# Leaving out the dummy matmuls that fill TensorE's waits in a two-block kernel

## The chip, the cores and the metric

The kernel runs on one NeuronCore of a Trainium2 chip, as one launch that computes the whole model. The metric is the device time of one execution in microseconds (us).
## The reference, cut to what matters

256 tokens of width 1024 pass through a first block of two layers and a second block of one layer. Between the parts stand RMS norms, and at those the matmuls have to wait, since each needs the norm of the whole row:

```python
for l in range(DEPTH):                       # first block, DEPTH = 2
    h = rmsnorm(x, g_mix[l])
    ... = jnp.split(h @ w_in[l], split_at, axis=-1)
    ...                                      # three kinds of attention
    x = x + jnp.concatenate([o_a, o_b, o_c], axis=-1) @ w_out[l]
    hf = rmsnorm(x, g_mlp[l])
    x = x + jnp.square(jax.nn.relu(hf @ w_ff1[l])) @ w_ff2[l]
x = rmsnorm(x, g_final)
# second block
p = rms_norm(x, norm1_gain) @ w_in
...                                          # attention, and the recurrent part (wkv7_scan)
o = (o + bonus) * g                          # end of the recurrent part
y_rwkv = o @ w_rwkv_out
mixed = gates[..., :D] * y_att + gates[..., D:] * y_rwkv
x = x + mixed @ w_out
x = x + hierarchical_moe(rms_norm(x, norm2_gain), ...)   # 32 experts, top 2
```

## The kernel before

Each engine has its own program, written out in order; semaphores tie them together. The two layers of the first block are a hardware loop (`for l`); the second block follows in straight code, and the experts (`hierarchical_moe`) are a last loop.

**A norm and its turn.** ScalarE takes the sums of squares (L1589, L1592), VectorE the reciprocals and the scaled rows (L2022, L2025), and signals `xn_ready` (`xn2_ready` in the second block). TensorE then turns the rows with 16 `transposes` (L965) into four PSUM banks (stages `tr1`, `tr2`, `tr3`). In the first block and at the entry of the second, ScalarE copies each bank out as a rounded high part (L1619) and VectorE forms the low part from it (L1633); `wait_emptied` makes TensorE wait for the last bank. Only then come the products.

**Split products.** The wide matmuls of the first block and of the second's projections are made of three passes (L984, L985, L986) over high and low parts of both operands. The weights' parts are made beforehand by ScalarE (L1645) and GpSimd or VectorE (L865), in queues that they share with the norms' work. The later matmuls of the second block, `token_major` (L974), are plain fp32; each fp32 matmul with a plain operand leaves two records in the trace.

**The filling.** `bridge(pe, units, key, n)` takes the bank of the stage named by `key` and issues n matmuls of 128x256 that read constants and whose result is overwritten by the stage's own first matmul (L956). They stand on TensorE's queue:

- in each layer ahead of `tr1` (18) and behind it (9), ahead of `tr3` (13) and behind it (4);
- at the entry of the second block, ahead of its `tr1` (28);
- ahead of `oT` (18), the turning of the recurrent part's result `o`, which waits for `o_ready`; `yrw`, the product with `w_rwkv_out`, follows;
- ahead of `mixT` (6), which waits for `mixed`; the product with `w_out` follows;
- ahead of `tr2` (10), the last norm; the router's small product `route`, the choice of experts on VectorE and the gathering of rows (L1517) follow, and then the experts' loop, whose first stage is `gate` (L1550).

A bridge has no semaphore of its own beyond the bank's: it is a fixed amount of work ahead of the wait, so TensorE looks at the wait only when the bridge is through. In all 88 matmuls stand in the two layers and 62 in the second block.

**The experts' weights.** The experts' matrices (2 MB each, `w_expert_gate`, `_up`, `_down`) go through single slots: SP issues the load of the next one (L941) when TensorE has finished the stage that read the slot.

Of the kernel before, what the change touches and what calls it, by code (L numbers as in the profile page):

```python
# [27 lines left out]
SEQ, D = 256, 1024  # L28
# [538 lines left out]
def program(nc, io, out):  # L567
    tables = shape_tables()
    with ExitStack() as ctx:
# [52 lines left out]
        def shared(name):  # L622
            o, w = shared_at[name]
            return shared_c[:, o:o + w]
# [9 lines left out]
        ident, causal = shared("ident"), shared("causal")  # L634
# [8 lines left out]
        proj = area(0, T * IN_W).rearrange("p (t w) -> p t w", t=T)  # L643
# [63 lines left out]
        oT = hTs[:, 1024:2048].rearrange("p (k s) -> p k s", k=4)  # L707
# [240 lines left out]
            sp.dma_start(out[0].rearrange("(t p) d -> p t d", p=P), x).then_inc(out_stored, 16)  # L948
            sp.wait_ge(out_stored, 16)

        def bridge(pe, units, key, n):

            bank = units.begin(key)
            for _ in range(n):
                pe.matmul(bank[:, 0:SEQ], ident, shared("causal")[:, 0:SEQ], start=True, stop=True)  # L956

        def transposes(pe, units, stage, src):

            for j in range(4):  # L960
# [17 lines left out]
        def _(pe):  # L978
# [39 lines left out]
            with pe.Fori(0, DEPTH) as l:  # L1018
                units = UnitView(LU, pe, psum, l)
# [72 lines left out]
                    if last_of_piece:  # L1092
                        read(("out", c, i), ins)

                bridge(pe, units, ("tr1", 0), 18)
                xn_ready.wait(pe, T, l)
                transposes(pe, units, "tr1", xn)
                bridge(pe, units, ("proj", 0), 9)
                units.wait_emptied(*(("tr1", j) for j in range(4)))
                for b in range(3):  # L1100
                    project_in(b, 0)
# [3 lines left out]
                for t in range(T):  # L1105
                    bank = units.begin(("idxT", t))
# [6 lines left out]
                for t in range(T):  # L1113
                    bank = units.begin(("dsaT", t))
# [19 lines left out]
                for t in range(T):  # L1134
                    bank = units.begin(("retT", t))
# [6 lines left out]
                for i, (t, s, h0) in enumerate(RET_UNITS):  # L1142
                    bank = units.begin(("retS", i))
# [12 lines left out]
                for t in range(T):  # L1156
                    bank = units.begin(("retO", t))
                    for h in range(RET_H):
                        mine = [i for i, u in enumerate(RET_UNITS) if (u[0], u[2]) == (t, h % 2)]
                        for i in mine:  # L1160
# [3 lines left out]
                                            start=(i == mine[0]), stop=(i == mine[-1]))  # L1164
# [15 lines left out]
                for j in range(4):  # L1180
                    t, c0 = j // 2, 4 * (j % 2)
                    bank = units.begin(("mlaT", j))
# [3 lines left out]
                for j in range(4):  # L1186
                    t, c0 = j // 2, 4 * (j % 2)
                    units.wait_emptied(("ukv", T * (j % 2) + t))
                    bank = units.begin(("mlaT", 4 + j))
# [8 lines left out]
                for g in range(N_DSA, NG + 2):  # L1198
# [4 lines left out]
                    n = g - N_DSA  # L1203
# [21 lines left out]
                for t in range(T):  # L1225
                    project_out(1, 0, t, range(4), t == T - 1)

                bridge(pe, units, ("tr3", 0), 13)
                xn_ready.wait(pe, 3 * T, l)
                transposes(pe, units, "tr3", xn)  # L1230
                bridge(pe, units, ("ff1", 0), 4)
                units.wait_emptied(*(("tr3", j) for j in range(4)))

                def ff1(b):
# [29 lines left out]
            units = UnitView(SU, pe, psum)  # L1264
# [6 lines left out]
            _, _, _, part2 = split_products(PW, units, hTp2, second_piece, 0)  # L1271

            def project(stage, blocks):
                for b, (_, w) in enumerate(blocks):
                    for i in range(4):
                        part2(stage, (stage, b, i), [(T * b, slice(0, w))], 2 * i, i == 0, i == 3)

            bridge(pe, units, ("tr1", 0), 28)
            pe.wait_ge(xn2_ready, T)
            transposes(pe, units, "tr1", xn2)  # L1280
            units.wait_emptied(*(("tr1", j) for j in range(4)))
# [4 lines left out]
            bank, r = units.begin(("bias", 0)), slice(0, BUCKETS + ATT_H)  # L1286
            units.finish(("bias", 0), pe.matmul(bank[0:ATT_H, 0:384], bias_tab[r, :], second("bucket_hot")[r, :],
                                                start=True, stop=True))
# [3 lines left out]
            for t in range(T):  # L1292
                bank = units.begin(("loraT", t))
# [5 lines left out]
            for t in range(T):  # L1299
                c = slice(t * P, (t + 1) * P)  # L1300
                for j, r in enumerate((slice(0, LORA_W), slice(LORA_W, P))):
                    bank = units.begin(("lora", 3 * t + j))
                    units.finish(("lora", 3 * t + j), pe.matmul(bank, loraT[r, 0, c], lora_w[r, 0, :], start=True, stop=True))
                bank, rest = units.begin(("lora", 3 * t + 2)), slice(0, LORA_G - P)
# [6 lines left out]
            for j in range(6):  # L1311
                bank = units.begin(("qkT", j))
# [6 lines left out]
            for i in range(NA + 2):  # L1319
                if i < NA:  # L1320
                    t, hg = ATT_UNITS[i]
                    bank, nk = units.begin(("S", i)), (t + 1) * P
                    r = slice(ATT_E * (hg % 2), ATT_E * (hg % 2 + 1))
                    per_bank = 512 // SEQ if t else GRP
                    for g0 in range(0, GRP, per_bank):
# [3 lines left out]
                        for g in range(g0, g1):  # L1329
                            c = (g * HPG + hg) // 2  # L1330
                            ins = pe.matmul(bank[:, g * nk:(g + 1) * nk], qT[r, c, t * P:(t + 1) * P], kT[r, c, 0:nk],
                                            start=False, stop=(g == g1 - 1))
                    units.finish(("S", i), ins)
                if 1 <= i <= NA:
                    t = ATT_UNITS[i - 1][0]
                    pe.wait_ge(att_exp, i)
                    bank = units.begin(("PT", i - 1))
# [123 lines left out]
                        ins = pe.matmul(o, bufK[:, 0, cols], pf[:, 0, C_V + c * P:C_V + (c + 1) * P], start=False, stop=True)  # L1461
                    units.finish(("state", 0), ins)

            bridge(pe, units, ("oT", 0), 18)
            pe.wait_ge(o_ready, 1)
            for j in range(2):
                bank = units.begin(("oT", j))
# [7 lines left out]
            for u in range(2 * T):  # L1475
                t, c = u // 2, u % 2
                token_major(pe, units, ("yrw", u), lambda k: oT[:, k, t * P:(t + 1) * P], w[:, :, c * 512:(c + 1) * 512])
            bridge(pe, units, ("mixT", 0), 6)
            pe.wait_ge(mixed, 1)
            transposes(pe, units, "mixT", gates[:, :, 0:D])  # L1480
            units.wait_emptied(*(("mixT", j) for j in range(4)))
# [2 lines left out]
                for t in range(T):  # L1484
                    token_major(pe, units, ("wout", T * c + t), lambda k: hT[:, k, t * P:(t + 1) * P], w)

            bridge(pe, units, ("tr2", 0), 10)
            pe.wait_ge(xn2_ready, 2 * T)
            transposes(pe, units, "tr2", xn2)
            units.wait_emptied(*(("tr2", j) for j in range(4)))  # L1490
# [1172 lines left out]
```

## Time and profile before

| | before |
|---|---|
| median of 3 runs | 1681.44 us |
| lowest, highest | 1679.95, 1683.43 us |
| the profiled execution | 1682.91 us, of which the span (first to last instruction) is 1681.1 us |
| mean granted clock of TensorE | 0.966 |
| TensorE busy | 1564.4 us (93%) |
| VectorE, ScalarE, GpSimd busy | 707.1, 539.6, 450.2 us |
| dummy matmuls (L956) | 150 matmuls, 300 records |
| DMA, last third of the span | about 428 GB/s, 9 tenths of the 16 DMA engines or more |

A row of a timeline is: start in us, duration in us, engine, source line, operation, output and inputs, and how many instructions the row merges; in brackets stands the idle time of that engine before the row and what ended it. The end of the last matmul of a row is modelled, so a spacing is better taken from starts.

### The profile page before, as it was taken

The numbers are of one execution on the slowest core, as the hardware profiler recorded it, in microseconds if no ns is written. First come the engines' busy times: TensorE is split into PE (matmuls) and PEld (weight loads), VectorE is DVE, ScalarE is ACT, GpSimd is POOL, SyncE is SP. The second block draws the span as 40 slices with busy tenths as digits, with TensorE's granted clock in tenths as the row PEclk, the third lists the DMA queues.
The fourth block names the chain that finished last, engine by engine and source line by source line (L and its number), as shares of the span: only waits on it lengthen the run. The fifth ranks groups of instructions, "written<-read, shape, count | busy, mean of one in ns | idle before, by whom it ended". The sixth has DMA issues, their size and how long they took to land.

```text
span 1681.1 us, 22339 instructions
## 1 busy us (share of the span) xinstructions
PE 1564.4 (93%) x8602; PEld 1156.4 (69%) x8602; DVE 707.1 (42%) x1087; ACT 539.6 (32%) x820; POOL 450.2 (27%) x159
## 2 busy tenths in 40 slices
PE   7979899999979999998989989999799999999997
PEld 6767799998768799986866769975453434344343
DVE  2866365563875365553145735721321111211112
ACT  4546433334646443333435431101111111111010
POOL 3453334333462333434887311100000000000000
PEclk9989999999999999998989999979899999999999
DMA  5432245533432255545654500003499999999994
GB/s 189 163 119 76 101 137 190 200 131 141 163 119 76 101 176 184 182 174 163 202 200 142 214 24 32 1 1 123 180 421 428 428 428 428 429 429 428 428 429 187
DMA packets 44547, 351.79 MB, mean 209 GB/s; under 512 B 5059, under 2 KB 7023, under 8 KB 19887
## 3 DMA queue, kind: packets, MB, share of 16 engines
q1 hardware_dynamic: 43774, 349.35, 54.1%
q8 instruction: 55, 0.90, 0.2%
q10 hardware_dynamic: 576, 1.12, 0.2%
q0 software_dynamic: 112, 0.17, 0.1%
q14 instruction: 30, 0.25, 0.0%
HBM read 347.70 MB, written 1.07 MB: 207 GB/s over the span
## 4 chain that ended last, share of the span: by engine, by line
PE 61%; DMA 18%; DVE 9%; issue 5%; ACT 3%; DVEq 2%; POOL 1%; ACTq 0%; SPq 0%; POOLq 0%
DMA ring<-in_w_expert_up 17%; PE psum L984 12%; PE psum L986 12%; PE psum L985 12%; PE psum L1550 8%; PE psum L974 3%; PE psum L956 1%; PE psum L1576 1%; DVE arena L2025 1%; PE psum L1517 1%; PE psum L1050 1%; PE psum L1419 1%; DVE arena L2070 1%; PE psum L1069 1%; DVE h_split L1633 1%
## 5 line engine op out<-in xcount | busy, mean ns | idle before, releaser
L865 POOL TENSOR_TENSOR weights_split<-weights_raw,weights_split 128x2048 fp32r<-128x2048 f32 (+4 forms) x108 | 392.2, 3644 | 470.6 <-ACT weights_split L1645 470.4
L1645 ACT ACTIVATE weights_split<-weights_raw 128x2048 fp32r<-128x2048 f32 (+5 forms) x156 | 243.5, 1565 | 327.2 <-PE psum L986 326.8
L1550 PE MATMUL psum<-ring,arena 128*64 128x512 f32 x1024 | 225.5, 593 | 25.8 <-DMA ring<-in_w_expert_up 24.7
L1550 PEld LDWEIGHTS psum<-ring,arena 128*64 128x64 f32 x1024 | 73.4, 137 | 174.6 <-issue 174.6
L984 PE MATMUL psum<-weights_split,h_split 128*128 128x512 f32 (+3 forms) x464 | 181.0, 390 | 9.6 <-DVE arena L2287 6.8
L986 PE MATMUL psum<-weights_split,h_split 128*128 128x512 f32 (+3 forms) x464 | 178.0, 384 | 0.0
L985 PE MATMUL psum<-weights_split,h_split 128*128 128x512 f32 (+3 forms) x464 | 177.7, 383 | 0.0
L984 PE MATMUL psum<-h_split,weights_split 128*128 128x256 f32 x512 | 145.0, 283 | 0.8 <-DVE h_split L1633 0.8
L986 PE MATMUL psum<-h_split,weights_split 128*128 128x256 f32 x512 | 144.9, 283 | 0.0
L985 PE MATMUL psum<-h_split,weights_split 128*128 128x256 f32 x512 | 144.9, 283 | 0.0
L984 PE MATMUL psum<-weights_split,hidden_split 128*128 128x512 f32 (+1 forms) x320 | 125.9, 393 | 13.7 <-DVE hidden_split L1633 13.7
L985 PE MATMUL psum<-weights_split,hidden_split 128*128 128x512 f32 (+1 forms) x320 | 125.0, 391 | 0.0
L986 PE MATMUL psum<-weights_split,hidden_split 128*128 128x512 f32 (+1 forms) x320 | 124.6, 389 | 0.0
L865 DVE TENSOR_TENSOR weights_split<-weights_raw,weights_split 128x2048 fp32r<-128x2048 f32 (+2 forms) x48 | 109.4, 2287 | 31.9 <-ACT weights_split L1645 31.2
L1576 PE MATMUL psum<-arena 128*64 128x512 f32 x512 | 113.4, 595 | 0.0
L984 PEld LDWEIGHTS psum<-weights_split,h_split 128*128 128x128 f32 x464 | 90.0, 194 | 29.4 <-issue 10.9
L986 PEld LDWEIGHTS psum<-weights_split,h_split 128*128 128x128 f32 x464 | 89.6, 193 | 17.6
L985 PEld LDWEIGHTS psum<-weights_split,h_split 128*128 128x128 f32 x464 | 89.9, 194 | 16.2
L984 PEld LDWEIGHTS psum<-h_split,weights_split 128*128 128x128 f32 x512 | 98.2, 192 | 2.1 <-issue 1.6
L985 PEld LDWEIGHTS psum<-h_split,weights_split 128*128 128x128 f32 x512 | 98.2, 192 | 0.5
L986 PEld LDWEIGHTS psum<-h_split,weights_split 128*128 128x128 f32 x512 | 98.2, 192 | 0.0
L2228 DVE TENSOR_TENSOR hidden_split<-arena,hidden_split 128x512 fp32r<-128x512 f32 x32 | 86.1, 2691 | 15.8 <-ACT hidden_split L1790 15.8
(354 smaller groups left out, 2157.3 us busy)
## 6 DMA issues: line engine op xcount, KB each, us to landing
weights_raw<-in_layer_w SPq DMA_DIRECT2D x94, 1024.0 KB, 4.8
ring<-in_w_expert_gate SPq DMA_DIRECT2D x32, 2048.0 KB, 16.1
ring<-in_w_expert_up SPq DMA_DIRECT2D x32, 2048.0 KB, 17.1
arena<-in_w_expert_down SPq DMA_DIRECT2D x32, 2048.0 KB, 13.4
weights_raw<-in_second_w SPq DMA_DIRECT2D x44, 512.0 KB, 4.3
weights_raw<-in_layer_w SPq DMA_DIRECT2D x6, 768.0 KB, 4.1
ring<-in_w_out SPq DMA_DIRECT2D x2, 2048.0 KB, 17.0
ring<-in_w_rwkv_out SPq DMA_DIRECT2D x1, 2048.0 KB, 9.7
```

The source lines that it names most:

```text
L865: eng.tensor_tensor(W.part(j, 1, n), W.raw(j, n), W.part(j, 0, n).bitcast(F32), ALU.subtract).then_inc(W.lo[W.pieces[j][1]], 1)
L956: pe.matmul(bank[:, 0:SEQ], ident, shared("causal")[:, 0:SEQ], start=True, stop=True)
L974: ins = pe.matmul(bank[:, 0:n], lhs(i), w[:, i, :], start=(i == 0), stop=(i == k - 1))
L984: pe.matmul(out, a[0], b[0], start=first, stop=False)
L985: pe.matmul(out, a[0], b[1], start=False, stop=False)
L986: return pe.matmul(out, a[1], b[0], start=False, stop=last)
L1050: pe.matmul(bank[:, j * nk:(j + 1) * nk], qT_, kT_, start=True, stop=False)
L1069: ins = pe.matmul(bank[:, j * MLA_V:(j + 1) * MLA_V], probsT[g % 2][:, c * P:(c + 1) * P], v, start=(s == 0), stop=(s == t))
L1550: ins = pe.matmul(bank[half(j), :], xe[h][:, k, half(j)], w[j][:, k, :], start=(k == 0), stop=(k == KD - 1))
L1576: ins = pe.matmul(bank[half(j), :], hidT[:, f, half(j)], w[j][:, f, c * 512:(c + 1) * 512], start=(f == 0), stop=(f == D_EXP // P - 1))
L1645: act.activation(W.part(j, 0, w), W.raw(j, w), ACT.Copy).then_inc(W.hi, 1)
L2228: dve.tensor_tensor(part[1], hid_sq[i % 4], part[0].bitcast(F32), ALU.subtract).then_inc(hid_ready.sem, 1)
```

## The change

Every call of `bridge`, and the function, are taken out. Nothing else is written differently: the waits, transposes and products stand in the same order, and the queues of the other engines hold the same instructions. TensorE is idle where the dummy matmuls were. (Line numbers behind the function shift by 7 and more in the changed kernel.)

```diff
-        def bridge(pe, units, key, n):
-            bank = units.begin(key)
-            for _ in range(n):
-                pe.matmul(bank[:, 0:SEQ], ident, shared("causal")[:, 0:SEQ], start=True, stop=True)
...
-                bridge(pe, units, ("tr1", 0), 18)
                 xn_ready.wait(pe, T, l)
                 transposes(pe, units, "tr1", xn)
-                bridge(pe, units, ("proj", 0), 9)
                 units.wait_emptied(*(("tr1", j) for j in range(4)))
...
-                bridge(pe, units, ("tr3", 0), 13)
                 xn_ready.wait(pe, 3 * T, l)
                 transposes(pe, units, "tr3", xn)
-                bridge(pe, units, ("ff1", 0), 4)
                 units.wait_emptied(*(("tr3", j) for j in range(4)))
...
-            bridge(pe, units, ("tr1", 0), 28)
             pe.wait_ge(xn2_ready, T)
...
-            bridge(pe, units, ("oT", 0), 18)
             pe.wait_ge(o_ready, 1)
...
-            bridge(pe, units, ("mixT", 0), 6)
             pe.wait_ge(mixed, 1)
...
-            bridge(pe, units, ("tr2", 0), 10)
             pe.wait_ge(xn2_ready, 2 * T)
```

TensorE's queue at the head of a layer, before: the loop's head, the bridge of 18, the transposes of the norm, the bridge of 9, and the first split product.

```order
L1018 UNCONDITIONAL_BRANCH
L956 MATMUL psum<-shared_c 128x256 x18
L215 ISA
L965 MATMUL psum<-shared_c,arena 128x128 x16
L956 MATMUL psum<-shared_c 128x256 x9
L129 ISA
L274 ISA
L984 MATMUL psum<-weights_split,h_split 128x512
```

The same place now (the transposes are L958, the products L977):

```order
L1011 UNCONDITIONAL_BRANCH
L1011 ISA
L958 MATMUL psum<-shared_c,arena 128x128 x16
L129 ISA
L274 ISA
L977 MATMUL psum<-weights_split,h_split 128x512
```

Only the two rows of L956 are gone; the transposes stand first, behind their wait.

TensorE's queue from the end of the recurrent part to the router, before (L1454 recurrent part, L1471 `oT`, L974 in turn `yrw`, `wout`, `route`):

```order
L1454 MATMUL psum<-arena 128x64
L956 MATMUL psum<-shared_c 128x256 x18
L1471 MATMUL psum<-shared_c,arena 128x128 x8
L974 MATMUL psum<-ring,hTs 128x512 x16
L956 MATMUL psum<-shared_c 128x256 x6
L965 MATMUL psum<-shared_c,arena 128x128 x16
L974 MATMUL psum<-ring,hTs 128x512 x32
L956 MATMUL psum<-shared_c 128x256 x10
L965 MATMUL psum<-shared_c,arena 128x128 x16
L974 MATMUL psum<-arena,hTs 128x36 x16
```

And now:

```order
L1442 MATMUL psum<-arena 128x64
L1458 MATMUL psum<-shared_c,arena 128x128 x8
L967 MATMUL psum<-ring,hTs 128x512 x16
L958 MATMUL psum<-shared_c,arena 128x128 x16
L967 MATMUL psum<-ring,hTs 128x512 x32
L958 MATMUL psum<-shared_c,arena 128x128 x16
L967 MATMUL psum<-arena,hTs 128x36 x16
```

Three rows of L956 are gone, and each set of transposes stands directly behind the products before it.

## Rows read from the trace of the kernel before

**Rows 1.** Timeline of SP: the first load that reuses an expert's slot.
```profile
1212.02 0.80 SPq L941 DMA_DIRECT2D ring<-in_w_expert_gate  x2
```
**Rows 2.** Chain that ended last: start us, us, what; in the experts' loop.
```profile
1273.90 21.58 DMA ring<-in_w_expert_up
```
**Rows 3.** TensorE by stretch: us, PE busy (instructions), granted clock, DMA share, GB/s.
```profile
202.00:203.00 1.00, 0.02 (x1) 0.80 0.46 74
206.00:207.00 1.00, 1.00 (x8) 0.99 0.01 0
208.50:388.00 179.50, 179.48 (x1153) 1.00 0.48 167
776.00:777.00 1.00, 0.00 (x0) 0.52 0.90 299
789.00:790.00 1.00, 1.00 (x4) 0.65 0.00 0
1117.00:1118.00 1.00, 1.00 (x5) 0.81 0.00 0
```
**Rows 4.** Timeline of all engines, first layer's `tr1`.
```profile
10.27 10.28 PE L956 MATMUL psum<-shared_c 128*128 128x256 f32 x36 [10.27 <-ACT causal_rounded L1656]
...
15.40 1.41 DVE L2025 TENSOR_SCALAR arena<-xs,stat 128x1024 f32<-128x1024 f32 x2
...
21.02 3.03 ACT L1619 ACTIVATE h_split<-psum,gains 128x256 fp32r<-128x256 f32 x8 [1.55 <-PE psum L965]
21.89 3.23 DVE L1633 SCALAR_TENSOR_TENSOR h_split<-psum,gains,h_split 128x256 fp32r<-128x256 f32 x8 [5.08 <-PE psum L965]
...
25.82 0.58 PE L984 MATMUL psum<-weights_split,h_split 128*128 128x512 f32 x1
```
**Rows 5.** Timelines of PE and ACT, second layer's `tr1`.
```profile
396.53 1.97 PE L965 MATMUL psum<-shared_c,arena 128*128 128x128 f32 x16 [0.55 <-DVE arena L2025]
...
403.58 0.39 PE L985 MATMUL psum<-weights_split,h_split 128*128 128x512 f32 x1
403.81 0.40 PE L986 MATMUL psum<-weights_split,h_split 128*128 128x512 f32 x1
...
399.03 3.00 ACT L1619 ACTIVATE h_split<-psum,gains 128x256 fp32r<-128x256 f32 x8
```
**Rows 6.** Timeline, first layer's `tr3`.
```profile
202.98 3.42 PE L965 MATMUL psum<-shared_c,arena 128*128 128x128 f32 x16 [2.96 <-DVE arena L2025]
...
208.52 0.38 PE L984 MATMUL psum<-h_split,weights_split 128*128 128x256 f32 x1 [0.39 <-DVE h_split L1633]
```
**Rows 7.** Timeline, entry of the second block.
```profile
778.31 3.67 PE L965 MATMUL psum<-shared_c,arena 128*128 128x128 f32 x16 [5.91 <-DVE arena L2025]
...
783.89 0.79 PE L984 MATMUL psum<-weights_split,h_split 128*128 128x512 f32 x1 [1.91 <-DVE h_split L1633]
...
784.48 0.63 PE L985 MATMUL psum<-weights_split,h_split 128*128 128x512 f32 x1
...
784.90 0.63 PE L986 MATMUL psum<-weights_split,h_split 128*128 128x512 f32 x1
```
**Rows 8.** Timeline, end of the recurrent part.
```profile
1113.62 9.87 PE L956 MATMUL psum<-shared_c 128*128 128x256 f32 x36
...
1121.73 0.69 DVE L2418 TENSOR_TENSOR arena<-arena 128x512 f32<-128x512 f32 x1
```
**Rows 9.** Timeline, ahead of `mixT`.
```profile
1138.96 2.75 PE L956 MATMUL psum<-shared_c 128*128 128x256 f32 x12
...
1142.29 1.97 PE L965 MATMUL psum<-shared_c,arena 128*128 128x128 f32 x16 [0.58 <-DVE arena L2472]
```
**Rows 10.** Timeline, last norm and router.
```profile
1172.67 4.48 PE L956 MATMUL psum<-shared_c 128*128 128x256 f32 x20
...
1178.09 1.97 PE L965 MATMUL psum<-shared_c,arena 128*128 128x128 f32 x16 [0.94 <-DVE arena L2025]
...
1181.08 3.73 PE L974 MATMUL psum<-arena,hTs 128*128 128x36 f32 x32 [1.01 <-ACT hTs L1601]
```

## What was predicted

> **What bounds the kernel now.** I read three views: the chain of waits, TensorE's busy time and clock by stretch, and the timeline around each dummy run. In the last third the chain goes alternately through a load of an expert's matrix and the matmuls that use it, with a wait of 21.6 us for each load [rows 2]: the loads set the time. But the run of loads without pause begins with one that SP issues at 1212.0 [rows 1], when TensorE has finished the first `gate` stage and frees its slot. So the tail is a block of fixed length hung on TensorE's path, and a microsecond lost anywhere on that path ahead of 1212 moves the end by one. Ahead of it TensorE is the bound: from the first product behind `tr3` to the layer's end it is busy 179.48 of 179.50 us [rows 3]. What the products lose there isn't caught by another wait. The dummies themselves are therefore of interest in two ways: where they keep TensorE from work that is ready (a gain when they go), and where they keep the clock up (a loss).
>
> **How the clock moves here.** Behind the dummies ahead of `tr3` TensorE stands idle for 2.96 us, and the clock falls 0.4 us before the transposes start (0.80 in the stretch 202 to 203), so about 2.6 us into the idle time [rows 3, 6]. At the entry TensorE is idle from 772.4 (5.91 before 778.31), and the clock falls at 776.0, after 3.6 us [rows 3, 7]. It comes back 3.0 us after the transposes of `tr3` start (206.0), 5.8 us after the first product at the entry (at 789.7, since 789 to 790 shows 0.65), and 3.8 us after the dummies at `oT` start (at 1117.4, since 0.81) [rows 3, 6 to 8]. A restart from the lower level thus costs 3.0 to 5.8 us of slow work; I take the mean of the three, **4.2 us**. The price of one such stretch: 512-wide split products start every 0.42 us in it, against 0.23 [rows 5, 7], so 1 - 0.23/0.42 = 0.45 of it is lost, 1.9 us (1.4 to 2.6). Plain fp32 products should lose half of it, 2.1 (1.5 to 2.9). Sixteen transposes take 3.42 to 3.67 us at the lower level and 1.97 at the upper [rows 5 to 7], 1.5 us more.
>
> **The change, place by place.**
>
> *First layer's `tr1` (18 and 9).* Here the dummies are in the way. The normed rows are ready at 15.40 + 1.41 = 16.8, but TensorE is in dummies until 20.55, and ScalarE idles 1.55 us for the transposes [rows 4]. Without them ScalarE starts at 21.02 - 1.55 = 19.5 (before that it is splitting weights), even with transposes at the lower level, which take from 16.8 to about 20.3, just ahead of its reading. VectorE ends at 25.12 now, the first product starts 0.7 later (25.82) since the nine dummies are still running [rows 4]; without them 0.1 later. Gain 1.55 + 0.6 = 2.1. Against it stands one slow stretch, 1.9: TensorE has been idle or slow ahead of it. Sum: **-0.2** (-2.1 to +0.5).
>
> *Second layer's `tr1`.* The transposes wait for the norm now (0.55 idle), so nothing is gained. Slow ones would end near 396.5 + 3.6 = 400.1; ScalarE begins to read at 399.03 and takes 3.00 for the four banks, so it reaches the last one at 401.3: hidden [rows 5]. If ScalarE's weight splitting did not stand there, they would cost the 0.5 to 1 us by which the first bank is later. The idle time from 388 to 396.5 and the gap behind the transposes leave the clock down. One slow stretch at the products: **+1.9** (1.4 to 2.6).
>
> *`tr3` in both layers (13 and 4).* The dummies ahead of it don't reach far enough: the transposes run at the lower level already [rows 6], and taking the dummies out leaves them as they are. What is new is the gap behind them, from 206.4 to 208.5, which four dummies filled, with the clock just back. Either the clock holds through these 2.1 us (0), or it falls again or never came back, and a slow stretch of 256-wide products follows. Their slow spacing is in no row; at half the clock they lose half at most: 2.1 (1.5 to 2.9). The three returns above lie at 3.0, 3.8 and 5.8 us of work, and the transposes offer 3.4, so it is rather the second. I take 1.5 for each layer, **+3.0** for both (0 to 5.8).
>
> On this the Trainium skill has a rule of its own: in "TensorE: Matmul & The Clock Gate", part 4 on the transpose, the full clock does not engage for transposes, since they don't count as busy work in the same way. This trace disagrees, for between 202.98 and the rise at 206.0 TensorE did nothing but transposes, at 0.50. By the rule both layers would pay the whole stretch.
>
> *Entry of the second block (28).* The longest run of dummies buys nothing here: it ends at 772.4, VectorE signals at 778.3, and clock, transposes and first products are slow already [rows 3, 7]. TensorE isn't awaited before 778.3. **0**, with 1.3 either way for how long the slow stretch is (3.0 instead of 5.8).
>
> *End of the recurrent part (18).* The clock is down when the dummies start (the rise comes at 1117.4) [rows 3, 8]. They end at 1123.49, and `o` is ready at 1122.42 [rows 8], so TensorE is some 0.9 late. Eight transposes at the lower level take 0.8 more, which eats that. Then the fp32 products of `yrw` start slow: **+2.1** (1.5 to 2.9). This is the surest loss, as nothing else lifts the clock here.
>
> *Ahead of `mixT` (6).* Idle time without the dummies: from about 1139.4 (the last product starts just before 1138.96) to 1142.29 [rows 9], so 2.9 us, between the 2.6 and the 3.6 at which the clock fell. If it falls, the four banks of transposes come 0.4 us apart more each, 1.3 in all at ScalarE's end, and a slow stretch, less what the transposes have already served of it, costs 1.9: 3.2 together. I take the fall, at 0.6. **+3.2** (0 to 4.2).
>
> *Ahead of `tr2` (10).* Idle from 1173.1 to 1178.09, 5.0 us [rows 10], beyond both falls: slow. The transposes cost 1.5. The router's 32 records take 3.73 now, 0.117 each, as quick as transposes at the upper level (1.97/16 = 0.123); at the lower level a transpose takes 0.214, which makes 0.09 x 32 = 2.9 at most. I take 2.2. Behind it VectorE's choice of experts hangs directly on the last result and moves along. **+3.7** (1.5 to 4.4).
>
> Sum: -0.2 + 1.9 + 3.0 + 0 + 2.1 + 3.2 + 3.7 = **13.7 us**. The profiled execution took 1682.9 (span 1681.1), 1.5 above the median of the runs; on the median the sum gives 1695.1, on the profile 1696.6. I say **1695**, 0.8% slower. The ends of the terms add up to +2 and +22, and won't all meet.
>
> A sentence of the Trainium skill bears on the size: the same page, part 1 on the clock gate, puts the whole ramp penalty at under 1% of a typical kernel's span, and says that the number of slow matmuls differs from run to run; the sum above is 0.8%, and the range below leaves room for such a spread.
>
> **The rivals.**
>
> *The clock needs less help than I think.* The transposes lift it in 3.0 us as in [rows 3, 6], it holds through the gaps behind them, and 2.9 us of idle time at `mixT` don't lower it. Then the `tr1` of both layers cost -2.1 and 0, `tr3` and `mixT` 0, and what is left is `oT` 2.1 and `tr2` 3.7: +3.7, so 1685, and up to 1690 if only some of it holds. For it: the row at 206.0. Against it: the entry, where 3.7 us of transposes didn't lift it [rows 3, 7]. Chance 0.22.
>
> *The transposes never count.* This is what the skill's rule makes of it, and it can be had from rows too: the entry's pattern (transposes slow, 5.8 us of slow products behind them) repeats at every place. Six stretches at 2.6 to 2.9 (both `tr1`, both `tr3`, `oT`, `mixT`) are 16.5, the transposes of `mixT` and `tr2` 2.8, the router 2.9, less 2.1 gained at the start: +20, so 1701.6. Chance 0.10.
>
> *Not slower: only the late dummies matter.* At the first `tr1` and at `oT` TensorE comes late to work that is ready, by 2.1 and 0.9 us in effect. If idle time didn't slow the matmuls behind it, these 3.0 us would be all: 1678.5. It decides where slow stretches are under 3.0/16.7 = a fifth of the size taken. The profile speaks against it with three slow restarts in its rows; there the clock figure goes with spacings of 0.42 against 0.23, so it isn't a label only. Chance 0.06 for anything from here up to no change, most of it short of a change that can be told.
>
> **How the numbers follow.** Forecast (1690 to 1700) 0.62, the first rival 0.22 (1685 to 1690), the second 0.10 (1700 to 1704), the third 0.06. The range 1686 to 1701 leaves out the third, the lower end of the first and about half of the second, somewhat under 0.2 in all. A measurement of this kernel tells 0.2% (3.4 us) from no change: slower than 1684.8 is 0.93, faster than 1678.1 0.01, between them 0.06.
>
> **What would show it right or wrong.** In the profile of the changed kernel: the first product some 2 us earlier, near 23.7; a granted clock of 0.50 at the first products behind both `tr1`, for 3 to 6 us each; at the entry the same rows as now, only shifted; `yrw` starting at 0.50; the first reused expert's slot loaded about 14 us later than 1212.0, and the same distance from there to the end as now (1681.1 - 1212.0 = 469.1). I am wrong if the clock stays at 1.00 behind the idle times, if that distance changes, so that the tail isn't a fixed block, or if TensorE shows waits for weights inside the layers that take up what is lost at their heads. The weakest terms are `mixT`, which hangs on 2.9 us of idle time, and `tr3`.

## The result, and the profile after

The changed kernel took 1698.74 us in the median of 5 runs (1695.38 to 1702.81), the kernel before 1681.44 (1679.95 to 1685.7, 5 runs on the same chip). The ratio is 1.0098, with a 95% interval of 1.0076 to 1.0120: slower by 17.3 us between the medians. The prediction was 1695, in a range of 1686 to 1701.

The profiled execution of the changed kernel has a span of 1697.5 us against 1681.1, and a mean granted clock of 0.944 against 0.966. From its page, the shares of the engines:

```profile
PE 1519.0 (89%) x8302; PEld 1114.1 (66%) x8302; DVE 712.0 (42%) x1087; ACT 539.6 (32%) x820; POOL 449.6 (26%) x159
```

TensorE issues the 300 records less and is busy 45 us less, and the kernel is longer. So the time lies in waits and slower matmuls. First the head of the first layer and of the second, from the timelines (start us, duration us, engine, line, what; answers to [rows 4] and [rows 5]):

```profile
16.87 3.67 PE L958 MATMUL psum<-shared_c,arena 128*128 128x128 f32 x16 [16.87 <-DVE arena L2010]
...
19.38 2.99 ACT L1604 ACTIVATE h_split<-psum,gains 128x256 fp32r<-128x256 f32 x8
...
23.60 0.49 PE L977 MATMUL psum<-weights_split,h_split 128*128 128x512 f32 x1 [3.06 <-DVE h_split L1618]
```

```profile
397.58 3.67 PE L958 MATMUL psum<-shared_c,arena 128*128 128x128 f32 x16 [8.42 <-DVE arena L2010]
...
404.29 0.79 PE L977 MATMUL psum<-weights_split,h_split 128*128 128x512 f32 x1 [3.04 <-DVE h_split L1618]
```

In the first layer ScalarE starts at 19.38 without an idle stretch and the first product comes at 23.60 instead of 25.82. In the second the transposes are slow, but that stays hidden: the first product starts 1.04 later than before (404.29 against 403.25), and TensorE was 1.05 behind already ahead of the transposes. The products then run slowly until 410.3. Then the `tr3` of the first layer, `oT`, `mixT` and `tr2` (to [rows 6] and [rows 8 to 10]):

```profile
202.55 3.38 PE L958 MATMUL psum<-shared_c,arena 128*128 128x128 f32 x16 [8.55 <-DVE arena L2010]
208.09 0.38 PE L977 MATMUL psum<-h_split,weights_split 128*128 128x256 f32 x1 [2.16 <-DVE h_split L1618]
```

```profile
1132.18 1.97 PE L1458 MATMUL psum<-shared_c,arena 128*128 128x128 f32 x8 [8.82 <-DVEq L2404]
1134.88 16.88 PE L967 MATMUL psum<-ring,hTs 128*128 128x512 f32 x32 [0.73 <-issue]
1154.93 3.35 PE L958 MATMUL psum<-shared_c,arena 128*128 128x128 f32 x16 [3.17 <-DVE arena L2457]
...
1191.95 3.60 PE L958 MATMUL psum<-shared_c,arena 128*128 128x128 f32 x16 [5.26 <-DVE arena L2010]
1196.57 5.02 PE L967 MATMUL psum<-arena,hTs 128*128 128x36 f32 x32 [1.02 <-ACT hTs L1586]
```

The same 32 records of `yrw` take 16.88 us; in the timeline of before they took 13.97:

```profile
1125.15 13.97 PE L974 MATMUL psum<-ring,hTs 128*128 128x512 f32 x32 [0.78 <-issue]
```

TensorE by stretch (us, PE busy, granted clock, DMA share, GB/s; to [rows 3]):

```profile
24.00:25.00 1.00, 1.00 (x5) 0.79 0.24 93
208.00:209.00 1.00, 0.92 (x7) 0.95 0.00 0
212.00:213.00 1.00, 1.00 (x9) 0.85 0.00 0
410.00:411.00 1.00, 1.00 (x5) 0.86 0.95 401
1140.00:1141.00 1.00, 1.00 (x3) 0.63 0.00 0
1154.00:1155.00 1.00, 0.07 (x1) 0.69 0.93 360
1157.00:1158.00 1.00, 1.00 (x7) 0.60 1.07 459
```

At the first layer's `tr1` the clock is up when the products start and falls at 24.6. At `tr3` the clock falls at 208.9, with the products under way for 0.8 us, and is back at 212.3. At `tr1` it is back at 410.3, at `oT` at 1140.7. At `mixT` it falls at 1154.4 and is back at 1157.8, before the products. SP's first load into a used expert's slot:

```profile
1228.70 0.80 SPq L941 DMA_DIRECT2D ring<-in_w_expert_gate  x2
```

That is 16.7 later than in [rows 1], and from it to the end of the span it is 468.8 us, against 469.1 before. The tail is a fixed block, and everything that was lost was lost ahead of it.

**Where it was lost.** Taking each start on TensorE against the same instruction's start in the trace of before, the lag grows like this (in us; e0 is the trace above, e10 the changed kernel's second trace, on another chip, further down; the last row holds what is left of the spans):

| stretch | e0 | e10 | predicted |
|---|---|---|---|
| first layer, `tr1` to the first `idxT` transposes (20.4 to 53.2) | -0.7 | +0.7 | -0.2 |
| second layer, `tr1` and the products behind it | +2.8 | +2.8 | +1.9 |
| `tr3` of both layers | +1.5, +1.5 | +1.5, +1.5 | +1.5, +1.5 |
| entry of the second block | -1.2 | -1.2 | 0 |
| `oT` and `yrw` | +3.0 | +2.9 | +2.1 |
| `mixT` | +1.2 | +1.2 | +3.2 |
| `tr2` and router | +2.9 | +2.9 | +3.7 |
| all else, mostly the middle of the second layer | +5.5 | +5.9 | 0 |

The places with bridges make +10.9 (e10: +12.3) where 13.7 were forecast. The rest comes from a stretch in which no bridge ever stood, the middle of the second layer, where the lag grows by 6.0. Of these, 3.4 come at one step: a product of TensorE waits for VectorE. Its row before, and in the changed kernel:

```profile
482.98 0.68 PE L984 MATMUL psum<-weights_split,hidden_split 128*128 128x384 f32 x1 [4.86 <-DVE hidden_split L1633]
...
490.06 0.68 PE L977 MATMUL psum<-weights_split,hidden_split 128*128 128x384 f32 x1 [8.24 <-DVE hidden_split L1618]
```

Timelines of VectorE and GpSimd at the last instruction of the key mask, of the kernel before and then of the changed one:

```profile
479.29 0.42 DVE L2087 SCALAR_TENSOR_TENSOR dsa_mask<-arena,shared_c 128x256 fp32r<-128x256 f32 x1
...
479.39 3.61 POOL L865 TENSOR_TENSOR weights_split<-weights_raw,weights_split 128x1536 fp32r<-128x1536 f32 x1 [1.36 <-ACT weights_split L1645]
```

```profile
483.11 3.67 DVE L2072 SCALAR_TENSOR_TENSOR dsa_mask<-arena,shared_c 128x256 fp32r<-128x256 f32 x1
...
483.09 3.42 POOL L865 TENSOR_TENSOR weights_split<-weights_raw,weights_split 128x1536 fp32r<-128x1536 f32 x1 [1.23 <-ACT weights_split L1630]
```

Where VectorE starts 0.1 us ahead of GpSimd's split it takes 0.42 us. Where it starts 0.02 behind, it takes 3.67 and ends with GpSimd's. Behind that stand two more slow stretches in which TensorE runs short matmuls between waits (2.6 us).

### The profile page after: what moved, and what is told of

Its sections match the earlier page's. It is cut to its first block, busy times and chain, and to the rows that moved or that the text cites. A ratio compares the mean times of both kernels' runs of the same rounds, so it can differ in the third digit from the quotient of the medians.

```text
span 1697.5 us, 21736 instructions
## 1 busy us (share of the span) xinstructions
PE 1519.0 (89%) x8302; PEld 1114.1 (66%) x8302; DVE 712.0 (42%) x1087; ACT 539.6 (32%) x820; POOL 449.6 (26%) x159
## 4 chain that ended last, share of the span: by engine, by line
PE 62%; DMA 15%; DVE 8%; issue 6%; POOL 3%; ACT 2%; DVEq 2%; ACTq 0%; POOLq 0%; SPq 0%
DMA ring<-in_w_expert_up 14%; PE psum L977 12%; PE psum L978 12%; PE psum L979 12%; PE psum L1535 9%; PE psum L967 3%; PE psum L1561 2%; POOL weights_split L865 2%; PE psum L1502 1%; DVE arena L2010 1%; PE psum L1043 1%; PE psum L958 1%; DVE h_split L1618 1%; PE psum L1407 1%; DVE arena L2055 1%
## 5 line engine op out<-in xcount | busy, mean ns | idle before, releaser
L977 PE MATMUL psum<-weights_split,h_split 128*128 128x512 f32 (+3 forms) x464 | 181.2, 391 | 13.8 <-DVE h_split L1618 8.1
L977 PE MATMUL psum<-h_split,weights_split 128*128 128x256 f32 x512 | 146.5, 286 | 4.3 <-DVE h_split L1618 4.3
L977 PE MATMUL psum<-weights_split,hidden_split 128*128 128x512 f32 (+1 forms) x320 | 126.4, 395 | 16.5 <-DVE hidden_split L1618 16.5
L977 PEld LDWEIGHTS psum<-weights_split,h_split 128*128 128x128 f32 x464 | 90.2, 194 | 34.8 <-issue 9.2
L977 PEld LDWEIGHTS psum<-h_split,weights_split 128*128 128x128 f32 x512 | 99.6, 195 | 5.2 <-issue 4.8
L978 PEld LDWEIGHTS psum<-h_split,weights_split 128*128 128x128 f32 x512 | 99.8, 195 | 0.5
L979 PEld LDWEIGHTS psum<-h_split,weights_split 128*128 128x128 f32 x512 | 99.7, 195 | 0.0
L958 PE MATMUL psum<-shared_c,arena 128*128 128x128 f32 x144 | 31.3, 407 | 74.1 <-DVE arena L2010 70.9
```

The costliest lines, as they stand in the source:

```text
L958: ins = pe.transpose(bank[:, kk * SEQ + t * P:kk * SEQ + (t + 1) * P], src[:, t, k * P:(k + 1) * P], ident)
L977: pe.matmul(out, a[0], b[0], start=first, stop=False)
L978: pe.matmul(out, a[0], b[1], start=False, stop=False)
L979: return pe.matmul(out, a[1], b[0], start=False, stop=last)
```

## The experiments

The numbers behind "lag" are as in the table above, from each run's own trace against that of before.

**e1 and e2: one block's bridges at a time.**

```diff
-                bridge(pe, units, ("tr1", 0), 18)
-                bridge(pe, units, ("proj", 0), 9)
-                bridge(pe, units, ("tr3", 0), 13)
-                bridge(pe, units, ("ff1", 0), 4)
```

> The kernel before without the four bridges of the first block's layers (18 and 9 at tr1, 13 and 4 at tr3); the second block keeps its four. Theory (clock restarts as summed place by place): the first layer's tr1 about -0.4, the second's +2.8, each tr3 +1.5, so +5.4 by places; in the middle of the second layer 0 to +6 more, where the changed kernel lost 5.8 us at a place without a bridge (a VectorE instruction of 0.4 us that took 3.7 beside GpSimd, and slow stretches). So 1685 to 1693. Rival (the loss sits in the second block, where the plain fp32 products are): within 2 us of the kernel before. Rival (the 5.8 us in the middle of the layer are a lasting consequence of the shift): 1691 to 1693 in every run.

```diff
-            bridge(pe, units, ("tr1", 0), 28)
-            bridge(pe, units, ("oT", 0), 18)
-            bridge(pe, units, ("mixT", 0), 6)
-            bridge(pe, units, ("tr2", 0), 10)
```

> The kernel before without the four bridges of the second block (28 at the entry, 18 at oT, 6 at mixT, 10 at tr2). Theory: 0 at the entry, +2.1 to 3.0 at oT, +1.2 to 3.2 at mixT, +2.8 to 3.7 at tr2, so +6 to +10: 1687.5 to 1691.5. If the losses of the parts add up, this and the run without the first block's bridges make together what the changed kernel lost, 16 to 17 us. Rival (one long restart counts, the others overlap with waits for VectorE): at most +4.

Without the first block's: 1.0049 (1.0031 to 1.0068). Without the second's: 1.0047 (1.0028 to 1.0066). Together 0.96%; the whole change cost 0.98% in its first measurement and 0.78% in its second (e10). The lags at the places without bridges are those of the table within 0.1 us (e1: second `tr1` 2.8, `tr3` 1.5 and 1.5; e2: `oT` 2.9, `mixT` 1.2, `tr2` and router 2.9), but for the first layer's `tr1`, which stands at +0.8 in e1. In the trace without the first block's bridges the hold-up of VectorE came in the second layer and not in the first, though both lie behind the same code; without the second block's, it came in the first.

**e3: the entry's bridge alone.**

```diff
-            bridge(pe, units, ("tr1", 0), 28)
```

> The kernel before without the bridge of 28 at the entry of the second block alone. Theory: that bridge ends 5.9 us before the wait does, the clock has fallen by then either way, so nothing changes: 1681.4, within 2 us; the transposes at the entry run at 0.50 in both, and only the length of the slow stretch behind them differs by chance (3 to 6 us). Rival (it still shortens the slow stretch, since it ended nearer to the restart): +1.5 to +3, with a longer slow stretch at the first products.

1.0001 (0.9988 to 1.0014). Timeline of TensorE at the entry, the answer to [rows 7]:

```profile
780.46 3.68 PE L965 MATMUL psum<-shared_c,arena 128*128 128x128 f32 x16 [17.96 <-DVE arena L2024]
786.04 0.79 PE L984 MATMUL psum<-weights_split,h_split 128*128 128x512 f32 x1 [1.91 <-DVE h_split L1632]
```

Idle for 17.96 us instead of 5.91, and from the transposes on the same rows: 3.68 against 3.67, the same 1.91, products back at full clock 5.9 us after the first (5.8 before). 28 matmuls bought nothing here, and they end 5.9 us ahead of the transposes; whether longer ones would have helped is tried in e6.

**e9 and e12: the short bridges behind the transposes, or the long ones ahead.**

```diff
-                bridge(pe, units, ("proj", 0), 9)
-                bridge(pe, units, ("ff1", 0), 4)
```

> The kernel before without the two short bridges that stand behind the transposes (9 behind tr1, 4 behind tr3); those ahead of the waits stay. Theory (the gap behind the transposes alone lets the clock fall): first tr1 -0.6 and perhaps a slow stretch of 1.3, second tr1 a gap of 4.7 us and a slow stretch of 1.5 to 2.8, tr3 +1.5 each as in the changed kernel: +4 to +6, so 1685.5 to 1687.5, which makes the 13 short matmuls worth as much as the 31 long ones ahead. Rival (the gaps ahead of the transposes make the loss, and 2 us behind them are too short): within 1.5 us of the kernel before.

```diff
-                bridge(pe, units, ("tr1", 0), 18)
-                bridge(pe, units, ("tr3", 0), 13)
```

> The kernel before without the two long bridges of the first block, 18 ahead of tr1 and 13 ahead of tr3; the short ones behind the transposes (9 and 4) stay. Theory (it is the gap behind the transposes that costs, since transposes count as work and lift the clock by themselves): tr3 0 to 0.5 each, the second tr1 0 to 1, the first tr1 -1.5 to +0.5; total -1 to +1.5. Rival (both are needed: the clock is down when the short bridge starts, and 4 to 9 matmuls are too few to lift it ahead of the products): +3 to +5.

Without the short ones: 1.0034 (1.0018 to 1.0050), and in the trace the same lags as without all four: second `tr1` +2.8, `tr3` +1.5 and +1.5. Without the long ones: 0.9996 (0.9977 to 1.0015), with +0.7 at the second `tr1` and none at either `tr3`. The timeline and the clock at the second `tr1`, without the long ones, show why:

```profile
390.77 3.68 PE L965 MATMUL psum<-shared_c,arena 128*128 128x128 f32 x16 [8.42 <-DVE arena L2023]
394.24 4.25 PE L956 MATMUL psum<-shared_c 128*128 128x256 f32 x18
398.14 0.58 PE L984 MATMUL psum<-weights_split,h_split 128*128 128x512 f32 x1
```

```profile
394.00:395.00 1.00, 1.00 (x6) 0.68 0.00 0
```

The transposes are slow after 8.42 us of idle time, and the clock is back at 394.6, just as they end and the nine matmuls begin (in the changed kernel, where nothing followed these transposes, it came back only under the products, at 410.3). The nine then stand in the gap, and the clock is still up at the products. They end 0.7 late, since the slow transposes made them start late, and that is the lag. So in a layer 13 matmuls in the gaps do what 44 were placed for. The rival of e12 is refuted at `tr1` and, by the lags of 0, at `tr3`.

**e7: bridges of transposes.** A helper that issues `pe.transpose` of 128x128 instead:

```diff
-            bridge(pe, units, ("tr1", 0), 28)
+            bridge_tr(pe, units, ("tr1", 0), 84)
...
-            bridge(pe, units, ("oT", 0), 18)
+            bridge_tr(pe, units, ("oT", 0), 60)
```

> The kernel before with two bridges made of transposes in place of matmuls: 84 of 128x128 at the entry of the second block (clock up when they start) and 60 at oT (clock down when they start). Theory (transposes count as work for the clock): at the entry the granted clock stays at 1.00 while they run, 84 x 0.12 = 10 us, and falls only in the idle time behind them; at oT it rises 3 to 6 us after they start. Rival (transposes don't count, as the Trainium skill's page TensorE: Matmul & The Clock Gate has it in part 4): at the entry it falls within 3 to 4 us though they run, and they then take 0.21 each, up to 17 us; at oT it stays at 0.50 for all of them, 60 x 0.21 = 13 us, and yrw starts slow and late, +3 us or more in the total.

One run, 1681.95. TensorE's timeline at `oT`, and the clock there and at the entry:

```profile
1112.86 8.40 PE L962 MATMUL psum<-shared_c 128*128 128x128 f32 x60
```

```profile
764.00:765.00 1.00, 0.95 (x9) 1.00 1.01 413
768.00:769.00 1.00, 0.00 (x0) 0.54 1.06 312
1116.00:1117.00 1.00, 1.00 (x10) 0.88 0.00 0
```

At the entry the clock is at 1.00 to the end of the 84 transposes (764.9) and falls 3.2 us into the idle time. At `oT` it rises 3.4 us after the first transpose (1116.2). Here transposes held the clock and lifted it. The statement of part 4 of the Trainium skill's page "TensorE: Matmul & The Clock Gate", which a rival of the prediction named, doesn't hold for these fp32 transposes.

**e4, e5 and e11: GpSimd's split out of VectorE's way.** GpSimd waits until the key mask is done:

```diff
                     for j in LW.lo_order["P"]:
                         if LW.index[first] <= j <= LW.index[last]:
+                            if j == LW.index["uq", 0, 2]:
+                                mask_ready.wait(pool, 1, l)
                             split_low(LW, pool, j, l)
```

> The kernel before, with GpSimd waiting for mask_ready ahead of the split of the weight piece (uq, 0, 2). Theory (a GpSimd tensor_tensor under way holds up VectorE's last two instructions of the key mask, which took 2.62 us instead of 0.29 in the first layer of the kernel before and 3.67 instead of 0.42 in the second layer of the changed one): both of them take 0.3 to 0.4 us in both layers; TensorE's product behind them starts 2.3 us earlier in the first layer, no change in the second; 1679. Rival (the long duration is the instruction's own, a late operand): they stay long where they were.

> The changed kernel, with GpSimd waiting for mask_ready ahead of the split of the weight piece (uq, 0, 2). In the trace of the changed kernel that split held up VectorE's last mask instruction by 3.0 us in the first and 3.2 us in the second layer. Theory A (the hold-up is a matter of chance from run to run and costs little in the median, as the same wait brought nothing in the kernel before): 1697 to 1700, the trace shows both instructions at 0.3 to 0.4 us. Theory B (leaving the bridges out shifts the engines so that the hold-up comes in every run, and it is a lasting part of the loss): 1691 to 1695.

> The changed kernel with GpSimd waiting for mask_ready ahead of the split of (uq, 0, 2), once more and against the changed kernel itself on the same chip. Theory B of its first run (the hold-up of VectorE by GpSimd's split belongs to the changed kernel's loss in most runs): 3 to 6 us below the changed kernel's median. Theory A (chance): within 1.5 us of it.

In all three traces both mask instructions take 0.29 or 0.30 and 0.42 or 0.43 us in both layers, so the cause of the long ones is GpSimd's instruction, and the rival of e4 falls. The second layer in e11, VectorE and then GpSimd:

```profile
479.74 0.30 DVE L2072 TENSOR_SCALAR arena<-arena 128x256 f32<-128x256 f32 x1
480.12 0.43 DVE L2074 SCALAR_TENSOR_TENSOR dsa_mask<-arena,shared_c 128x256 fp32r<-128x256 f32 x1
...
480.70 3.43 POOL L865 TENSOR_TENSOR weights_split<-weights_raw,weights_split 128x1536 fp32r<-128x1536 f32 x1 [1.84 <-DVE dsa_mask L2074]
```

The times: for the kernel before 1.0003 (0.9993 to 1.0012), no gain, where 2 us were expected. For the changed one 1695.1 (e5), at 1.0065 (1.0040 to 1.0089) of the kernel before, and the second time 1693.58 (1692.33 to 1694.44, 6 runs) beside the changed kernel's 1696.14 (1693.49 to 1701.3, 6 runs). That is 2.6 us less, between the two theories, and their ratios to before overlap, 1.0062 (1.0045 to 1.0078) and 1.0078 (1.0058 to 1.0098). So the gain of the wait is likely but not shown. Nor does the wait make the times steady: with it the changed kernel's runs spread over 2 us in e11 and over 9 in e5 (1691.16 to 1700.4), without it over 8.

**e10: the changed kernel again.** No edit; the partner of e11.

> The changed kernel once more, as the partner of the next one on the same chip. The same ratio as before, +1.0% (+0.75 to +1.2), and at each place without a bridge the same loss as in its first trace, within 0.5 us: first tr1 -2.2 at the first product and +1.5 to 2.7 behind it, second tr1 +2.8, tr3 +1.1 to 1.6 each, oT +2.9, tr2 +2.9; mixT 0 or +1.2.

1.0078 (1.0058 to 1.0098), 13.3 us between the medians (1696.14 and 1682.89), and the lags of the table. Its trace has both hold-ups (3.62 and 3.65 us).

Over the nine traces without the extra wait (before, changed, e1, e2, e3, e7, e9, e10, e12; sized bridges apart) a mask instruction was held up in the first layer of five and in the second of six. The first has it in those of before (2.62 us), changed, e2, e9 and e10; the second in those of changed, e1, e3, e9, e10 and e12. The changed kernel (both of its traces) and e9 have it in both layers; e1, whose first block is that of the changed kernel, in one. Before, e2, e3 and e7 have one and the same first block, and differ: the first layer only, the first only, the second only, neither. So it is a race that goes either way from run to run, and whether the change makes it worse is not settled. In e3, whose layers are those of before, the second layer loses the same 3.4 and 2.5 us as in the changed kernel.

**e6 and e8: bridges that fit their waits.**

```diff
-                bridge(pe, units, ("tr1", 0), 18)
+                bridge(pe, units, ("tr1", 0), 16)
-                bridge(pe, units, ("proj", 0), 9)
+                bridge(pe, units, ("proj", 0), 8)
-                bridge(pe, units, ("tr3", 0), 13)
+                bridge(pe, units, ("tr3", 0), 19)
-                bridge(pe, units, ("ff1", 0), 4)
+                bridge(pe, units, ("ff1", 0), 6)
-            bridge(pe, units, ("tr1", 0), 28)
+            bridge(pe, units, ("tr1", 0), 40)
             pe.wait_ge(xn2_ready, T)
             transposes(pe, units, "tr1", xn2)
+            bridge(pe, units, ("rw", 0), 6)
-            bridge(pe, units, ("oT", 0), 18)
+            bridge(pe, units, ("oT", 0), 16)
-            bridge(pe, units, ("mixT", 0), 6)
+            bridge(pe, units, ("mixT", 0), 7)
-            bridge(pe, units, ("tr2", 0), 10)
+            bridge(pe, units, ("tr2", 0), 11)
```

> The kernel before with the bridges sized to the waits that its trace shows: tr1 16 instead of 18 and 8 instead of 9, tr3 19 instead of 13 and 6 instead of 4, entry 40 instead of 28 and a new one of 6 behind its transposes, oT 16 instead of 18, mixT 7 instead of 6, tr2 11 instead of 10. Theory (what counts is whether the clock is up when the products start and whether TensorE comes late): transposes of tr3 and of the entry at 1.00 and some 0.5 us earlier each, first products at the entry without a slow stretch (-2.7), oT 0.9 earlier, first tr1 0.6 earlier, so about -5: 1676 to 1678. Rival (dummies raise the clock no further than they did): 1681 to 1683.

> The kernel before with the bridges sized to their waits, as in the run of that name, and GpSimd's wait for mask_ready in addition. Theory: the sized bridges bring 3 to 4 us against the kernel before, the wait nothing to 1 us more, since it brought nothing to the kernel before; 0.9975 to 0.998 of it. Rival (the two hold-ups, where they come, cost 3 us each): 0.996.

The sized bridges: 1679.79 beside 1683.16 (12 and 24 runs), 0.9979 (0.9967 to 0.9991), faster than both kernels, with 3.4 us gained where some 5 were expected. With GpSimd's wait as well 0.9982 (0.9970 to 0.9994), the same. TensorE at the entry, sized bridges:

```profile
776.31 1.97 PE L965 MATMUL psum<-shared_c,arena 128*128 128x128 f32 x16 [0.74 <-DVE arena L2026]
...
781.32 0.50 PE L984 MATMUL psum<-weights_split,h_split 128*128 128x512 f32 x1 [0.45 <-DVE h_split L1634]
781.66 0.39 PE L985 MATMUL psum<-weights_split,h_split 128*128 128x512 f32 x1
781.89 0.40 PE L986 MATMUL psum<-weights_split,h_split 128*128 128x512 f32 x1
```

Transposes of 1.97, products every 0.23 from the start; against the trace of before the entry gives back 3.2 us and `oT` 0.8, while the router takes 1.8 more, since the clock falls 1.7 us into it. e7 loses 1.9 at the router too, with the code of before there, so this is not the sizing's doing. The entry is also the direct test of the price of a restart: the same place, once with the clock down and once up, differs by 2.7 behind the first product.

## Why the prediction was right

**The frame held.** The loss sits ahead of the experts' loop, the tail kept its length (468.8 for 469.1), and nothing inside the layers caught the slow products up. The forecast of the total was 4 us low against the first measurement (17.3 us lost) and level with the second (13.3, for 13.7 forecast). In the traces it is right partly by luck, because two errors offset each other: the places with bridges cost less than forecast, and 5.5 us that were in no term of the sum came on top.

**The price of a restart was too small at two places.** The mean of three stretches was 4.2 us; the stretches behind the first product of the second `tr1` and of `yrw` were 6.0 and 5.9 us, which makes 2.8 and 2.9 lost where 1.9 and 2.1 stood. Behind the second `tr1` the stretch is 5.9 to 6.0 in every trace without the short bridge. Behind `oT` it is 5.6 to 5.9 in four traces (changed, e2, e10, e11), but 3.8 in e5, where the same code starts at 1132.50 and the clock is back at 1136.3; that costs 1.9:

```profile
1136.00:1137.00 1.00, 1.00 (x3) 0.86 0.00 0
```

So the price of the same restart differs from run to run within the prediction's 3.0 to 5.8 or a little beyond. At `oT` the 0.8 that the missing dummies give back and the 0.9 that slow transposes take met as worked out. The entry's row (5.8) was the like case, with work that starts after a long idle time; the two shorter stretches, of 3.0 and 3.8, came from rows in which transposes or dummies without a gap did the lifting.

**`mixT` was mis-sized, and is the worst term: 3.2 taken, 1.2 measured.** The clock did fall, at 1154.4, as bet. But the step "a slow stretch, less what the transposes have already served of it" took 1.9 for that stretch, and it was nothing: the clock was back at 1157.8, a microsecond before the products at 1158.96. The prediction had the row for it (the return within 3.0 us of transposes) and used it for `tr3` only. In e5 the clock didn't fall there, with the same 3.17 us of idle time, and the lag was 0: the bet on the fall was won in four traces of five.

**`tr3` was right in size.** 1.5 for 1.5 taken, in both layers. How it comes about is told by e9 and e12: the gap behind the transposes does it, not the one ahead. It was written as either holding or falling; here it did both, the transposes bring the clock back and it falls again with the products under way for 0.8 us (208.9). So the size was partly luck: the sum took something between two cases, and a third came.

**First `tr1`**: the gain came as worked out (first product 2.2 earlier) and was given back behind it: net -0.7 in one trace, +0.7 in the other. The sign isn't the change's: e2, e3 and e7, whose first block is that of before, stand at +0.5, -0.4 and -0.7 there. Nor was the clock at 0.50 from the first product on in both, as foretold: in the first trace it fell 1.0 us behind it. **`tr2`**: 1.6 for the transposes, 1.4 for the router where 2.2 were taken; the router's 32 records took 5.02, since the clock had come back 1.2 us ahead of it (1195.4) and fell again 2.2 us into it (1198.8). **Entry**: 0 was right for the bridge itself (e3). The -1.2 in the changed kernel isn't the bridge's: it appears without the first block's bridges as well (e1). There the clock is up when the products start, falls 1.1 us behind and is back 4.5 us behind, so 3.4 us are slow instead of 5.8; the prediction had these rows unchanged.

**What wasn't in the sum**: 6.0 us in the middle of the second layer. 3.4 of them are the hold-up of a VectorE instruction by GpSimd, shown by e4, e5 and e11 to be that; the other part goes with TensorE's clock between short matmuls, and came with and without the hold-up (e11 has 2.5 there too). The trace of before happened to be free of both in its second layer, and e3 has both with the same code. Against the medians the hold-up counts for less than in the traces (2.6 us in e11, nothing in e4), so part of these 6.0 is the luck of one trace and not a cost of the change. How much was not separated. With the hold-ups gone the changed kernel lost 10.7 us (e11) and 11.9 (e5), near the 10.9 of the places.

**The rivals.** That the clock needs less help than thought: true in part. The transposes lifted the clock at `tr3`, `mixT` and `tr2`, and it held from there to the products. But at the second `tr1` they didn't lift it, at `tr3` it fell again 0.8 us into the products, and the idle time at `mixT` did lower it in four traces of five. That transposes never count: refuted by e7. That only the late dummies matter: its gains are real (2.2 at the first product, 0.8 at `oT`), but the slow stretches came.

## What to carry to other kernels

In this kernel, filling a wait with dummy matmuls paid only where it reached the work behind the wait: compare its end with the time at which the wait ends, and look at the gap between the transposes and the first product as well as at the one ahead of them. Real transposes brought the clock back by themselves in most places, so a few matmuls behind them (13 of 44) carried what gain could be measured, and a long run that ended early (28) carried none. In a trace, price a restart by a row with the same idle time ahead of it, and check a second trace before a microsecond or three in a busy stretch is put down to the change.

## What the runs showed of the hardware that was not expected

A VectorE instruction with both inputs in SBUF took 3.48 to 3.69 us instead of 0.42 when a GpSimd `tensor_tensor` had begun 0.01 to 0.24 us ahead of it (0.02 in the lines above, 0.24 in the first layer of the same trace), and it ended within about 0.3 us of GpSimd's. Begun ahead of GpSimd's by as little as 0.01 (e1, 102.79 against 102.80) or 0.13 (e2, second layer), it took 0.42 or 0.43. A one-input instruction was held up too (2.62 us for 0.29, first layer of before), while the searches for maxima beside the preceding GpSimd split were not. The Trainium skill's page "GPSIMD Engine Reference", in its table of the engine's specifications, says that the two share their SBUF interfaces and that instructions of VectorE in a two-port mode or with two SBUF inputs contend; these traces agree for the two SBUF inputs; whether the one-input instruction ran in a two-port mode no row says. The price in these rows was the whole rest of GpSimd's instruction, of 3.42 us in most, for a VectorE instruction of 0.42.
